# A diffusion trunk step in which the 128 context tokens get a token mixer of their own, and their expert rows are gathered while the 512 latent tokens are mixed

## What is computed

```
def trunk_layer(x, mod, l, p, ctx):
    sh_a, sc_a, g_a, sh_f, sc_f, g_f = jnp.split(mod.astype(x.dtype), 6, axis=-1)
    h = x * (1.0 + sc_a) + sh_a
    mix, new_ctx = token_mixer(h, l, p, ctx)      # h @ w_in (11 x 1024 + 3 x 1024 columns), three branches, gates, w_out
    x = layer_norm(DEEPNORM_ALPHA * x + g_a * mix, p['ln_g'][0], p['ln_b'][0])
    h = x * (1.0 + sc_f) + sh_f
    ff = peer(h, p['peer_wq'], p['peer_keys'], p['peer_u'], p['peer_v'])
    x = layer_norm(DEEPNORM_ALPHA * x + g_f * ff, p['ln_g'][1], p['ln_b'][1])

def peer(...):  # per token: 8 heads, each chooses 16 of 16384 experts
        ue = jnp.take(u_tab, idx, axis=0)
        ve = jnp.take(v_tab, idx, axis=0)
        act = jax.nn.gelu(jnp.einsum('td,thkd->thk', xb, ue).astype(jnp.float32), approximate=False)
        return jnp.einsum('thk,thkd->td', (g * act).astype(ve.dtype), ve)
```

## Time and profile before

| | |
|---|---|
| time, median of 3 runs | 6493.6 us (6487.25 to 6494.71) |
| profiled execution, its own time | 6495.05 us |
| its span, first to last instruction | 6493.2 us |
| granted TensorE clock, mean | 0.974 |
| PE busy | 5624.4 us (87%) |
| DVE busy | 3986.4 us (61%) |
| ACT busy | 2574.1 us (40%) |
| POOL busy | 1565.5 us (24%) |
| DMA | 1633.04 MB, 252 GB/s over the span |

### The profile page before, as it was taken

The page is one execution under the profiler, slowest core; times in us unless marked ns, Lnnn a source line. Parts: engine busy times, 40 slices in busy tenths (PEclk is TensorE's granted clock), DMA queues, the critical chain, the costliest instruction groups (busy, mean ns, idle before and its releaser), DMA issues. The chain is left out here.

```text
span 6493.2 us, 98870 instructions
## 1 busy us (share of the span) xinstructions
PE 5624.4 (87%) x37464; PEld 3994.9 (62%) x37464; DVE 3986.4 (61%) x8297; ACT 2574.1 (40%) x6132; POOL 1565.5 (24%) x1625
## 2 busy tenths in 40 slices
PE   7989999898888888878799899998988888888886
PEld 7878999788433343433388799997874343333332
DVE  3556244456777777777836552355667677776777
ACT  2665112241444444444427541123324444444444
POOL 0330000002333333333304300000023333333332
PEclk8999999999999999999999999999989999999999
DMA  4011212333999999999920121213249999999998
GB/s 186 9 49 67 78 66 83 115 119 143 419 421 420 420 414 415 415 420 412 418 114 11 44 79 67 77 70 131 76 188 421 421 419 416 419 418 411 419 412 358
DMA packets 241004, 1633.04 MB, mean 252 GB/s; under 512 B 27168, under 2 KB 49120, under 8 KB 64100
## 3 DMA queue, kind: packets, MB, share of 16 engines
q0 software_dynamic: 184320, 1342.26, 50.0%
q1 hardware_dynamic: 56214, 284.46, 11.8%
HBM read 1611.68 MB, written 17.56 MB: 251 GB/s over the span
## 5 line engine op out<-in xcount | busy, mean ns | idle before, releaser
L2152 PE MATMUL ex_ps_y<-ring,peer_small 128*128 128x512 f32 x2272 | 1100.4, 620 | 272.5 <-ACT peer_small L2103 270.5
L2152 PE MATMUL ex_ps_y<-early,peer_small 128*128 128x512 f32 x2272 | 1085.7, 612 | 253.1 <-ACT peer_small L2103 251.2
L2152 PEld LDWEIGHTS ex_ps_y<-ring,peer_small 128*128 128x128 f32 x2272 | 413.0, 194 | 895.1 <-issue 894.6
L2152 PEld LDWEIGHTS ex_ps_y<-early,peer_small 128*128 128x128 f32 x2272 | 410.9, 193 | 871.0 <-issue 869.7
L1989 DVE CUSTOM_DVE_ANT_0 early<-early,ex_ps_h 128x1024 f32<-128x1024 f32 x568 | 693.4, 1221 | 412.2 <-DMA early<-in_peer_uv,ex_index 407.9
L1989 DVE CUSTOM_DVE_ANT_0 ring<-ring,ex_ps_h 128x1024 f32<-128x1024 f32 x568 | 693.2, 1220 | 388.3 <-DMA ring<-in_peer_uv,ex_index 384.1
L2095 ACT ACTIVATE ex_act<-ex_dot 128x1 f32<-128x1 f32 x1280 | 256.9, 201 | 1582.8 <-DVE ex_dot L1989 1581.8
L1677 POOL DMA_INDIRECT ring<-in_peer_uv,ex_index x568 | 546.1, 961 | 912.7 <-PE ex_ps_y L2152 824.1
L1677 POOL DMA_INDIRECT early<-in_peer_uv,ex_index x568 | 546.2, 962 | 899.0 <-PE ex_ps_y L2152 788.3
L2103 ACT ACTIVATE peer_small<-ident,ex_w 128x128 f32<-128x128 f32 x1280 | 514.1, 402 | 41.9
L2099 ACT ACTIVATE ex_w<-ex_act,ex_share 128x1 f32<-128x1 f32 x1280 | 376.9, 294 | 46.7 <-ACT ex_act L2095 0.4
(11 more groups left out here) (362 smaller groups left out, 13282.4 us busy)
## 6 DMA issues: line engine op xcount, KB each, us to landing
ring<-in_w_in SPq DMA_DIRECT2D x54, 2048.0 KB, 8.5
ring<-in_mod_w SPq DMA_DIRECT2D x22, 2048.0 KB, 8.0
ring<-in_w_branch SPq DMA_DIRECT2D x12, 2048.0 KB, 8.5
room<-in_peer_wq SPq DMA_DIRECT2D x14, 1024.0 KB, 25.3
ring<-in_peer_uv,ex_index POOLq DMA_INDIRECT x568, 17.2
early<-in_peer_uv,ex_index POOLq DMA_INDIRECT x568, 17.2
ring<-in_w_out SPq DMA_DIRECT2D x4, 2048.0 KB, 8.5
x_rows<-main SPq DMA_DIRECT2D x10, 512.0 KB, 7.1
```

The source lines that it names most:

```text
L2152: last = nc.tensor.matmul(ps_y[n % 2][:, c:c + 512], diag[s % DIAGS], v_row[slot(n, s)][:, c:c + 512], start=s == 0, stop=s == TOPK - 1)
```

## The change

The latent tokens and the context tokens part. TOK becomes 512 and NB 4, so all stages above handle the latent tokens alone. Ahead of them each layer gets new stages for the 128 context tokens:

- `context_in`: 32 chunks of weights (in layer 0 also 8 of the modulation, which leave the attention core of layer 0), loaded anew into four buffers and multiplied in plain float32 without splitting (`context_chunk`), with attention and convolution of the context in between;
- a forward and a backward `scan` of one block (`latent=False`);
- `context_out`: merge, output projection, normalisation, and all queries and scores of the context's experts.

The choice of the context's experts, its gathers, dots and sums are no stage of their own. `projections` gets a parameter `behind`: a fixed number of pieces of foreign work that DVE (and in one stage POOL) does after each tile (`hooks`). The choosing lies in `rf0`, 24 dots in `rf1`, 56 in `recm`, 48 dots and 48 sums in `conv`, 52 sums in `qkv`, 28 in `attm`. Each u row and each v row is gathered by itself (4 KB a token, 512 KB in all) into one of five buffers. The sum over v is made by DVE, not by PE. Then `context_end` finishes the context's layer, and `experts` serves the latent blocks alone: 32 units, with SLOTS = 10. The attention core has 32 units, all with 640 keys. Before, layer 0's core made 8 modulation pieces of layer 0 and 4 of layer 1, and layer 1's core the other 8; now `context_in` of layer 0 makes the first 8, layer 0's core all 12 of layer 1, and layer 1's core none.

```diff
-TOK = LAT + CTX
+TOK = LAT
 NB = TOK // P
...
-SLOTS = 9
+SLOTS = 10
...
-def projections(nc, name, jobs, ring, ident, beside=None, then=None):
+def projections(nc, name, jobs, ring, ident, beside=None, then=None, behind=None):
+    def hooks(n, t):
+
+        return range(t * n // len(tiles), (t + 1) * n // len(tiles))
...
-                        spans = [(512 * b, slice(TOK // 2 * b, TOK // 2 * (b + 1))) for b in range(2)]
+                        spans = [(0, slice(0, TOK))]
...
-                                cols = TOK // 2 if job.channel_major else HALF
+                                cols = TOK if job.channel_major else HALF
...
                         if job.after_on == "vector":
                             dve.wait_ge(slot_free[t % 4], t // 4 + 1)
                             job.after(steps, m, e)
+                        for j in hooks(behind.n_vector, t):
+                            behind.vector(dve, j)
                     if half_of[r] + 2 < n_halves:
                         dve.wait_ge(tile_done, done_through[r])
                         split(half_of[r] + 2)
...
                         job.after(step, m, e)
                     beside.pool_after_tile(pool, step, t)
+                    for j in hooks(behind.n_pool, t):
+                        behind.pool(pool, j)
+                behind.pool_all(pool)
                 beside.pool_last(pool, step)
...
+CTX_SLOTS = 5
+PICKS = 16
+DOTS = 24, 56, 48
+SUMS = 48, 52, 28
+U_FIRST, V_FIRST = DOTS[0] + DOTS[1], SUMS[0]
+PHASES = (("u", 0, U_FIRST, (0, 1, 2, 3, 4)), ("u", U_FIRST, CHOICES - U_FIRST, (2, 3, 4)),
+          ("v", 0, V_FIRST, (0, 1)), ("v", V_FIRST, CHOICES - V_FIRST, (0, 1, 2, 3, 4)))
...
+    def gather(self, pool, side, j):
+        s, n, behind = LANDINGS[side, j]
+        if side == "u":
+            pool.wait_ge(self.picked, self.base_picks + PH * PICKS + 1)
+        if behind is not None:
+            pool.wait_ge(self.dotted if side == "u" else self.added, self.l * CHOICES + behind)
+        pool.sem_inc(self.going, 1)
+        index = self.index_u if side == "u" else self.index_v
+        self.nc.gpsimd.indirect_dma_start(self.row(s), None, self.table, bass.IndirectOffsetOnAxis(
+            ap=index[:, j:j + 1], axis=0)).then_inc(self.landed[s], 16)
+
+    def dot(self, dve, j):
+        s, n, behind = LANDINGS["u", j]
+        dve.wait_ge(self.landed[s], 16 * (self.l * LANDED[s] + n))
+        self.nc.vector.tensor_tensor_reduce(out=self.row(s), in0=self.row(s), in1=self.h[:], scale=1.0, scalar=0.0, op0=ALU.mult,
+                                            op1=ALU.add, accum_out=self.dots[:, j:j + 1]).then_inc(self.dotted, 1)
...
+        dve.wait_ge(self.added, self.l * CHOICES + j)
+        V.scalar_tensor_tensor(self.y[:], self.row(s), w, self.y[:], ALU.mult, ALU.add).then_inc(self.added, 1)
...
+class FirstDots(Behind):
+
+    n_vector, n_pool = DOTS[0], DOTS[0] + CTX_SLOTS
...
+class DotsAndSums(Behind):
...
+    def pool_all(self, pool):
+        for j in range(DOTS[2]):
+            self.experts.gather(pool, "u", U_FIRST + j)
+            self.experts.gather(pool, "v", j)
...
+def context_chunk(nc, ps, kind, w, x):
+
+    if kind in ROW_KINDS:
+        for k in range(KT):
+            last = nc.tensor.matmul(ps[:, 0:CHUNK], x[:, k, :], w[:, k, :], start=k == 0, stop=k == KT - 1)
+        return last
+    for m in range(CHUNK // P):
+        for k in range(KT):
+            last = nc.tensor.matmul(ps[:, m * P:(m + 1) * P], w[:, k, m * P:(m + 1) * P], x[:, k, :], start=k == 0, stop=k == KT - 1)
+    return last
...
+    order = [(kind, c) for kind in ("ZQ", "ZK", "ZV", "ZC", "ZX", "ZB", "RQ", "RI", "RFF", "RFB", "RG", "G0", "B0", "G1", "B1", "G2") for c in range(2)]
+    if l == 0:
+        for j in range(MOD_CHUNKS - FIRST_CHUNKS):
+            order.insert(5 + 4 * j, ("mod", FIRST_CHUNKS + j))
...
+                for p in range(4, len(order)):
+                    kind, c = order[p]
+                    sp.wait_ge(tile_done, p - 3)
+                    sp.dma_start(bufs[p % 4], context_weights(T, l, kind, c)).then_inc(w_in_s[p % 4], 16)
...
+                recurrent_branch(nc, l, T, h_split, main, by_token(rooms[0]), by_token(rooms[1]), ring, ident, (Choosing(E), FirstDots(E)), E.y)
+                recurrent_out(nc, l, T, h_split, by_token(rooms[0]), by_channel(rooms[1]), main, ring, ident, MoreDots(E))
+                conv_branch(nc, l, T, h_split, rooms[0], rooms[1], main, ring, ident, DotsAndSums(E))
+                attention(nc, l, T, h_split, by_token(rooms[0]), by_token(rooms[1]), ring, ident, Sums(E, s1, SUMS[1], True))
+                attention_out(nc, l, T, h_split, by_token(rooms[0]), by_channel(rooms[1]), main, by_token(rooms[1]), norm, rows, ring, ident, Sums(E, s2, SUMS[2]))
+                context_end(nc, l, T, h_ctx, ident, E)
```

1194 lines of the change are left out of this document (924 added, 270 removed).

## The result

The changed kernel takes 6454.6 us (median of 7 runs, 6448.9 to 6476.1) beside 6494.7 us for the kernel before (7 runs, 6487.3 to 6501.8): a ratio of 0.9941, 95% interval 0.9931 to 0.9952. It is faster, by 0.6% and clear of the spread of its runs, but by 40 us and not by the 139 of the forecast. The median lies within the stated range of 6250 to 6465, which is wide, and outside the likeliest case (6300 to 6412).

A forecast was written before the change was run, and what follows sets the result against it. PE bounds the projection stages, DMA the experts. Layer 0: context mixer +473, latent mixer -180, experts -332, so -39; layer 1: +448 - 216 - 332 = -100; together -139, median 6355 us, range 6250 to 6465.

The forecast's parts named there:

- the likeliest case: Whole kernel: the forecast itself, 6355 us, with 6300 to 6412 given a chance of 0.58.
- the scans' sum: The context mixer's two scans of one block: 47 us each, 94 a layer.
- signs of being wrong: DVE idle over 0.2 us before each context row, dots over 1.22 us, `context_in` idle for weights, a latent stage no shorter.
- +11 by guess: `conv`: with two v buffers and gathers of 0.94 + some 3.5 us, some additions come before their row, +11 us.
- the last dot's landing in `rf1`: `rf1`: the last dot follows its landing by 5 us, part of the 84 us.
- landings on DVE's path: Each of 512 context-row visits waits; no faster from a 0.27 us mean wait, 6590 us at 0.5; chance 0.09.
- for which I add 8: `rf1`: POOL operations wait for the end of DVE operations with two SBUF inputs, 8 us of the 84.
- The start: `rf1`: gathers wait for the shares of the experts, some 8 to 10 us into the stage.
- the surplus terms in `recm`, `conv` and `qkv`: DVE work beyond PE's: late low parts in `recm`, +12 and +4 us in `conv`, 146 against 134 in `qkv`.
- The rival built on it: `rf1`, `recm`, `conv`: DVE and gathers exclude each other, 0.94 us of DVE per gather, 6575 us; chance 0.06.
- the better cover: PSUM slots and lead absorb DVE's surplus, short POOL waits: `rf1`, `recm`, `conv`, `qkv` -60 a layer, 6235 us; chance 0.14.

The follow-up runs named there:

- the best version: Changed kernel with all dots before additions in `conv`, no dots in `rf1` (64 each in `recm` and `conv`), more additions in `qkv` and `attm`: 6382.7 us (0.9831).

## Why the prediction was wrong in its size

**Right.** The direction; the experts (1391 and 1377 us, DMA share 0.97 and 0.98); the pitch of the 512-column matmuls and so the floors of all latent stages; `context_in` (260 and 244 for 265 and 245); the four latent scans (109, 115, 105, 112 for 110 each); the attention core (166 and 126 for 170 and 124); that POOL bounds `rf1`; that `conv` is the tightest on DVE. The context's two scans took 81 us for 94, `context_out` 94 to 96 for 88. That the median fell into the stated range owes something to luck: the scans' sum was too high by 13 and 12 us, and without that the kernel would have come out above it. Two of the signs of being wrong that the forecast named came true, a mean wait of over 0.2 us before each context row and dots longer than 1.22 us (1.38 in `rf1`).

**Wrong, and where.** The step that failed is the price of the moved work on the stages that carry it. Over the floors the forecast charged 35 us in `rf1` (84 for 49), 17 in `recm`, 24 in `conv`, 6 in `qkv` and less than nothing in `attm`, some 80 us a layer. The runs charge 135: by stage 47, 20, 36, 21 and 10 in layer 0. By its own terms:

- "+11 by guess", the additions that come before their row, and the last dot's landing in `rf1`, but no term for the other dots: the waits for landings cost 40 us a layer. The guess took a way of 0.94 + 3.5 us from the load of a state. The gathers of the context land 5.2 us after issue in `rf1` and 5.6 to 6.3 in the other stages, and DVE waits for them 211 us in all (158 at dots, 24 at additions, and 30 more at additions that the view puts down to no releaser but that end with a landing), of which 80 reach the end. The rival "landings on DVE's path" named the mechanism and priced it wrongly: its threshold of a mean wait of 0.27 us took each wait as paid in full. The mean is 211 / 512 = 0.41 us, and the kernel is still faster, since more than half of the wait does not reach the end: it falls into DVE's slack.
  The page's group of dots (busy us, mean ns, idle before them), and then the gathers' issues (median us from issue to landing; those of v have 5.9):

```profile
L2313 DVE CUSTOM_DVE_ANT_0 ctx_rows<-ctx_rows,ctx_h 128x1024 f32<-128x1024 f32 x256 | 318.3, 1253 | 158.5 <-DMA ctx_rows<-in_peer_uv,ctx_iu 157.9
```

```profile
ctx_rows<-in_peer_uv,ctx_iu POOLq DMA_INDIRECT x256, 5.8
```

- "for which I add 8" in `rf1`: POOL's waits for DVE came to 14 us there. The start was 13 us in place of 8 to 10, and 6 us lie between POOL's last gather and the next stage.
- The barriers behind stages with gathers were in no term: POOL's DRAIN adds some 17 us a layer to the four stages from `rf1` to `qkv`, by the time from the last work of a stage to the next stage, with gathers and without. That is part of the gathers' 84 us.
- DVE's own work: 53 us a layer, where the surplus terms in `recm`, `conv` and `qkv` come to some 40. In `recm` and `conv` it was less than forecast (8 and 7 for 16 each), in `rf1`, `qkv` and `attm` more (13, 12, 10). I had compared sums of busy time, DVE 146 and PE 134 in `qkv`, and taken the larger, and in `attm` DVE's 122 lay under PE's 134. But the last pieces run on after PE's last matmul. In `qkv`:

```profile
1539.86 1.29 DVE L2337 SCALAR_TENSOR_TENSOR ctx_y<-ctx_rows,ctx_dots,ctx_y 128x1024 f32<-128x1024 f32 x1 [0.73 <-DMA ctx_rows<-in_peer_uv,ctx_iv]
...
1541.97 2.70 DVE L2337 SCALAR_TENSOR_TENSOR ctx_y<-ctx_rows,ctx_dots,ctx_y 128x1024 f32<-128x1024 f32 x2 [0.48 <-DMA ctx_rows<-in_peer_uv,ctx_iv]
1549.72 0.16 DVE L894 TENSOR_TENSOR att_neg_lam<-att_lam 128x1 f32<-128x1 f32 x1 [5.06 <-PEq L90]
```

PE's last products of `qkv` begin at 1534.7, DVE ends at 1544.7, and the next stage begins 5 us after that, of which 4.3 are POOL's DRAIN. Ending the foreign work earlier gained nothing, though, so I take the tail for a symptom of the amount and not for a cost of its own.

- The clock was in no term of these stages. PE ran at 1.00 in `rf1` and at 1.00 in `conv` and `qkv` before; now it is 0.79, 0.95 and 0.95. In `conv` PE runs at the lower level for 3.4 us after four of its waits for low parts in each layer (those of 1.8 to 3.7 us; two others of 1.7 and 2.3 us had none behind them), each time at a loss of some 1.7 us, as in the timeline above. That is 7 us beside 15 and 18 us of waits. It is part of the 270 us and not on top of them; in the other stages its share was not read, and no run measures it by itself.

**The exclusive port.** The rows show both halves. Dots in `conv`, where POOL only issues gathers, take 1.218 us in the mean over 48, and 1.219 without gathers, so DVE loses nothing to gathers, while the gathers take 1.20 and 1.41 us for 0.94. It is DVE that lengthens them: of the 96, the 11 with no DVE instruction beside them take 0.94 us in the mean, the 64 beside a dot or an addition 1.26, and the 15 beside another operation with two SBUF inputs, mostly low parts, 1.89, up to 2.88. In `rf1`, beside refinings, DVE loses too: without gathers its 24 dots take 1.715 us in the mean, and the refinings go from 0.86 to 1.50.

```profile
L2307 DVE CUSTOM_DVE_ANT_0 ctx_rows<-ctx_h 128x1024 f32<-128x1024 f32 x24 | 39.7, 1715 | 0.0
```

By the rule of the Trainium skill (SBUF — State Buffer, "SBUF: two separate sides"), that two SBUF inputs on DVE and a reading GpSimd operation exclude each other for the whole instruction, this is what the refinings should do, and the trace agrees. The rival built on it charged 0.94 us of DVE's time for each gather and gave 6575; the gathers' whole presence costs 84 us, and in `conv` they take none of DVE's time. Of the 21 to 30 us of it that lie outside `rf1`, POOL's DRAINs take some 24, so POOL's later issuing and the traffic of the rows cost little in those stages as long as nobody waits for a landing. The forecast's own figures for these rivals had two slips that change nothing: the gathers of the three stages are 176, not 181, and the gains of the better cover add up to 64 us a layer, not 60.

## What to carry to other kernels

Work that is moved beside a bound engine is not free up to the sum of busy times: each piece cost 0.37 us in `conv` on the average and 2 us at the margin, though DVE was busy for only 205 of 264 us. With its 50 us of waits for rows it was full. Price moved work by its waits too: if an in-order engine takes rows from a transfer, put the latency of that very transfer in that traffic into the sum, and ask how much slack swallows it. And first look which stage has a third engine as its bound: 24 dots in `rf1` with their gathers cost 42 us, since POOL had to issue the gathers between its own operations, and half the dots still cost 26; moving all of them elsewhere gave 35 of the 72 us that the best version gains over the change. And look at the barriers: if a stage has got a new kind of work, compare the time from its last instruction to the next stage with what it was.
